# Products ahead of the transposes in each step of the first stack's attention

## The reference

```
proj = rms_norm(h, g_mix[l]) @ w_in[l];  q, k, v, xr, gr = split(proj)
# 4 heads, each with two score maps c = 0, 1 of head size 64; rotary on q and k
s = q_c @ k_c.T * 64**-0.5, causal;  pr = softmax(s)
attn = pr[0] - lam * pr[1];  o = attn @ v;  o = rms_norm(o, g_subln) * (1 - lam_init)
y = rg_lru(conv(xr)) * gelu(gr)                       # the recurrent half
h = h + concat([o, y]) @ w_out[l]
h = h + square(relu(rms_norm(h, g_mlp[l]) @ w_mlp_in[l])) @ w_mlp_out[l]
gate = sigmoid(rms_norm(h, g_ple[l]) @ w_ple_gate[l]);  h = h + gate * (p[l] @ w_ple_proj[l])
```

## Time and profile before

| | |
|---|---|
| median of 3 runs | 2460.05 us (2459.33 to 2461.67) |
| the profiled execution: its time | 2455.17 us |
| its span, first to last instruction | 2453.4 us |
| PE busy | 2394.1 us, 98% |
| PEld busy | 1937.7 us, 79% |
| DVE busy | 1362.2 us, 56% |
| ACT busy | 895.8 us, 37% |
| share of PE in the chain that ended last | 89% |
| attention steps of layer 0, 136.00 to 204.00 us: PE, DVE, ACT busy | 62.37, 45.33, 39.10 of 68.00 us, granted clock 1.00 |

### The profile page before, as it was taken

How to read it: one execution, slowest core, us unless ns; L and a number is a source line. 1 busy time by engine, 2 the same in 40 slices (tenths; PEclk the granted TensorE clock), 3 DMA queues, 4 the chain that set the end, 5 groups by cost and what they waited for, 6 DMA issues and landing times.

```text
span 2453.4 us, 28925 instructions
## 1 busy us (share of the span) xinstructions
PE 2394.1 (98%) x11498; PEld 1937.7 (79%) x11498; DVE 1362.2 (56%) x1976; ACT 895.8 (37%) x1299; POOL 349.9 (14%) x270
## 2 busy tenths in 40 slices
PE   8999999999999999999999999999999999999997
PEld 6877888888887788888876878888886877888886
DVE  7775433445777543344578876344357975633433
ACT  4555332234355533223432354223243244321331
POOL 2002000001200200000246521000012832000002
PEclk9999999999999999999999999999999999999998
DMA  4311222222231222222221221222221211222221
GB/s 158 107 57 69 98 91 103 91 98 86 102 109 56 74 102 87 103 94 89 91 91 69 69 84 59 103 93 95 102 104 57 87 52 70 81 91 103 91 97 51
DMA packets 33181, 215.56 MB, mean 88 GB/s; under 512 B 4145, under 2 KB 4401, under 8 KB 8113
## 3 DMA queue, kind: packets, MB, share of 16 engines
q1 hardware_dynamic: 33072, 214.08, 24.4%
HBM read 211.97 MB, written 2.10 MB: 87 GB/s over the span
## 4 chain that ended last, share of the span: by engine, by line
PE 89%; DVE 7%; ACT 2%; issue 1%; POOL 1%; DMA 0%; SPq 0%; POOLq 0%; DVEq 0%; ACTq 0%
PE ps L426 81%; DVE wl L366 1%; PE ps L2225 1%; PE ps L2178 1%; DVE gl L648 1%; PE ps L2249 1%; PE ps L2239 1%; PE ps L1389 1%; PE ps L606 1%; PE ps L1413 1%; PE ps L309 1%; PE ps L1376 1%; ACT wh L360 0%; PE ps L2228 0%; DVE x L1340 0%
## 5 line engine op out<-in xcount | busy, mean ns | idle before, releaser
L426 PE MATMUL ps<-gh,wh 128*128 128x512 f32 x1488 | 589.4, 396 | 13.6 <-DVE gl L648 11.0
L426 PE MATMUL ps<-gh,wl 128*128 128x512 f32 x1488 | 581.0, 390 | 0.0
L426 PE MATMUL ps<-gl,wh 128*128 128x512 f32 x1488 | 580.9, 390 | 0.0
L426 PE MATMUL ps<-hh,wh 128*128 128x512 f32 x1456 | 575.1, 395 | 3.0 <-ACT arena L964 1.1
L360 ACT ACTIVATE wh<-wr 128x2048 fp32r<-128x2048 f32 x184 | 351.1, 1909 | 594.9 <-PE ps L426 594.5
L426 PE MATMUL ps<-hh,wl 128*128 128x512 f32 x1456 | 567.3, 390 | 0.0
L426 PE MATMUL ps<-hl,wh 128*128 128x512 f32 x1456 | 567.0, 389 | 0.0
L366 DVE TENSOR_TENSOR wl<-wr,wh 128x2048 fp32r<-128x2048 f32 x168 | 387.1, 2304 | 277.8 <-ACT wh L360 275.5
L426 PEld LDWEIGHTS ps<-gh,wh 128*128 128x128 f32 x1488 | 279.3, 188 | 82.1 <-DVE gl L648 13.5
L426 PEld LDWEIGHTS ps<-hh,wh 128*128 128x128 f32 x1456 | 272.9, 187 | 68.3 <-issue 8.0
L426 PEld LDWEIGHTS ps<-gh,wl 128*128 128x128 f32 x1488 | 279.5, 188 | 59.7
(11 more groups left out here) (264 smaller groups left out, 2445.8 us busy)
## 6 DMA issues: line engine op xcount, KB each, us to landing
wr<-in_weights SPq DMA_DIRECT2D x195, 1024.0 KB, 4.8
out_yt<-x SPq DMA_DIRECT2D x8, 256.0 KB, 2.0
x<-in_xt SPq DMA_DIRECT2D x3, 512.0 KB, 7.9
wr<-in_weights SPq DMA_DIRECT2D x2, 512.0 KB, 5.8
arena<-in_gates SPq DMA_DIRECT2D x2, 512.0 KB, 7.7
arena<-in_embed SPq DMA_DIRECT2D x2, 512.0 KB, 5.3
par<-in_params_b SPq DMA_DIRECT2D x2, 274.0 KB, 2.7
x<-in_xt SPq DMA_DIRECT2D x2, 256.0 KB, 4.1
```

The costliest lines, as they stand in the source:

```text
L426: done = pe.matmul(out, stationary, moving, start=(first and n == 0), stop=(last and n == 2), skip_group_check=True)
```

## The change

In the loop over the 16 steps, PE's `recurrent_tile` or `projection_tile` is issued ahead of `turn(s)` (and of `turn_back`) instead of behind them. `scores(s+2)` stays first, `weigh(s-1)` last. The loop stands in the program of both first-stack layers. Nothing on the other engines changes its order.

```
         for s in range(STEPS):
             if s + 2 < STEPS:
                 scores(s + 2)
-            turn(s)
-            if s % QT == 3 and s > QT:
-                turn_back(s // QT - 1, s - 1)
             if s < KT:
                 recurrent_tile(s)
             else:
                 projection_tile(s - KT)
+            turn(s)
+            if s % QT == 3 and s > QT:
+                turn_back(s // QT - 1, s - 1)
             if s:
                 weigh(s - 1)
         weigh(STEPS - 1)
```

## The result

The changed kernel takes 2470.54 us (median of 5 runs, 2469.24 to 2471.19), the one before 2459.33 us (median of 5 runs, 2456.95 to 2461.67). The ratio is 1.0043, with a 95% interval of 1.0032 to 1.0054: slower by 8 to 13 us. Repeated on two chips, beside new runs of before, the same kernel gave 1.0034 twice (1.0021 to 1.0046, and 1.0022 to 1.0045). Forecast were 2468.5 us (a loss of 8.4) and a range of 2463.5 to 2473.

A forecast was written before the change was run, and what follows sets the result against it. PE, busy for 98% of the span, was taken as the bound. Per layer -5.1 - 0.96 - 0.07 + 5.9 + 3.7 = +3.5 us; two layers +7.1, with new neighbours +8.4, on 2460.05 gives 2468.5 us, range 2463.5 to 2473.

The forecast's parts named there:

- Part 1: At PE's transposes of the mixed probabilities: all waits for DVE's mix go, saving 5.1 us per layer.
- Part 2: At weigh in steps 7, 11, 15: PE stands 1.96 us each while bank 7 is emptied, 5.9 us per layer.
- rival 2: Faster: in steps 7, 11, 15 the bank 7 chain shrinks below 0.9 us; 2452.5 us, chance 0.04.
- Part 3: Projection tiles in steps 10, 11, 14, 15 wait for ACT's copy of an earlier tile: 3.7 us per layer.
- Rival 1: Only bank 7 costs, the projection copies stay hidden: +1.0 us, 2461 us, chance 0.12.
- Part 4: Transposes now ahead of 128x128 work in all 32 steps: 0 to 0.08 us each, 1.3 us taken in all.
- The sum: Both layers' steps: +3.5 us per layer, +7.1 for two, +8.4 us with the cost of new neighbours.
- slower by over 0.2%: Whole kernel: the outcome of a loss above 4.9 us, given a chance of 0.81.
- within 0.2%: Whole kernel: the outcome of a difference under 4.9 us, hard to tell from no change, chance 0.15.
- Rival 3: ACT sets the pace from step 8 on: 0.4 us for 8 steps per layer, +6.4 more, 2475 us, chance 0.09.
- Nothing later takes it up: Behind the steps: PE is bound by itself and no transfer depends on it, so the 8.4 us loss stays whole.

The follow-up runs named there:

- experiment 1: Changed kernel, but steps 7, 11 and 15 keep the old order, transposes ahead of products; 2459.74 us against 2459.16 before, ratio 1.0003.
- experiment 5: Kernel before with its PE order, but turn_back ahead of turn, and ACT's output_high and keep_projection ahead of untangle; 2456.44 us, ratio 0.9983.
- experiment 3: Changed kernel with turn_back ahead of the products in steps 7, 11, 15 and ACT's output_high ahead of untangle; 2455.72 us, ratio 0.9985.
- experiment 2: Changed kernel with ACT's keep_projection ahead of untangle instead of at the end of its step; 2467.30 us, ratio 1.003.
- experiment 4: Changed kernel with turn_back ahead of the products, and ACT's keep_projection, then output_high, ahead of untangle; 2452.84 us, ratio 0.9975, later 2453.85, ratio 0.9964.
- experiment 6: Changed kernel with turn_back ahead of the products in steps 7, 11 and 15, ACT's order left as it was; 2477.54 us, one run.
- the kernel filled in part: Changed kernel plus unread matmuls: 7 behind turn_back, 4 ahead of the projection tiles of steps 14 and 15; 2467.44 us, unfilled copy 2470.83.

## Why the prediction was right

**Part 1, waits that go (5.1 us per layer).** Right: no wait of L1401 is left in either layer. Experiments 1 and 5 bring it back exactly where the old order is.

**Part 2, bank 7 (1.96 us in each of three steps).** Right: 2.31 us from L1422 to L1413 again, less 0.35, with brackets of 1.71. Experiment 1 gives the three steps their old order and the loss is gone, experiment 3 hides the chain and 6.1 us per layer come back (75.11 to 69.02). The chain did not shrink, so rival 2 is refuted: no piece of it had been lateness.

**Part 3, the projection's copy (3.7 us per layer).** Right in place and size. Lost from start to start: step 10, 183.59 - 182.83 - 0.09 = 0.67 (0.65 was forecast); step 11, 0.45 (0.5); step 14, 200.42 - 198.87 - 0.31 = 1.24 (1.35); step 15, 203.96 - 202.24 - 0.54 = 1.18 (1.2). Together 3.5 us. The 0.09 is what the mask matmul now leaves to L426 where PE doesn't wait. Rival 1, in which these copies stay hidden, is refuted by experiment 2, whose brackets vanish.

**Part 4, new neighbours (1.3 us in all).** The steps in which PE waits for nothing measure it. The first scores of steps 1 and 2 in the changed kernel:

```profile
140.93 1.13 PE L1389 MATMUL ps<-arena 64*128 64x512 f32 x4
...
145.48 0.49 PE L1389 MATMUL ps<-arena 64*128 64x128 f32 x4
```

and before:

```profile
140.25 1.13 PE L1389 MATMUL ps<-arena 64*128 64x512 f32 x4
...
144.75 0.49 PE L1389 MATMUL ps<-arena 64*128 64x128 f32 x4
```

4.55 us instead of 4.50. In the same way steps 0, 2, 4, 5 and 6 are longer by 0.07, 0.05, 0.06, 0.08 and 0.01. The half of 0.08 that was taken is about right. The 0.08 itself was read from two groups that both stood behind a wait, but it holds where PE waits in neither kernel: two transposes take 0.14 us ahead of a 128x512 matmul (141.44 to 141.58, before) and 0.22 ahead of other 128x128 ones (144.94 to 145.16, changed), three take 0.26 and 0.33. Some 0.03 of it comes back behind the mask matmuls.

**The sum.** Forecast for the steps 8.4 us, measured 7.9 us. The chances don't follow from their own rule: 0.75 less a tenth of it, and 0.09, is 0.77 for "slower by over 0.2%" where 0.81 stands, and 0.19 is left for "within 0.2%" instead of 0.15. Rival 3 is refuted: scores wait once per layer for ACT, as before, and L1401 not at all.

**What the sum left out.** "Nothing later takes it up" named PE as bound by itself behind the steps, and took its speed as given. It is not: in each of the three traces of the changed kernel the granted clock falls behind the steps, in at least one layer. The medians are 11.2, 10.6 and 9.2 us above before in three comparisons, the means 11.2, 9.1 and 8.6: 0.7 to 3.3 us more than the steps. The range held this because the bounds of the other terms were wide, not because the clock was thought of; for this part it was luck.

That the rest is the clock can be read from the timed runs, since each has its mean granted clock on record. The 63 runs of before spread from 2455.2 to 2463.5 us, and the time follows the clock: 0.994 in the fast ones, 0.989 or 0.990 in the slow ones. Call (1 - clock) x time what a run loses by the clock, about 20 us in before. A straight line through all 157 timed runs that have a clock, with a level of its own for each kernel in each comparison, gives 0.67 us of time for each us of this loss. At equal clock the kernels then lie where their steps put them, to about 0.5 us (the clocks on record are rounded to 0.001, which is 2.5 us in one run, and the first set of the changed kernel is set against all runs of before, since those beside it have no clock on record):

| | from before, at equal clock | twice the stretch's difference |
|---|---|---|
| changed, three sets of runs | +7.9, +8.3, +7.9 | +7.9 |
| experiment 1 | +0.1 | +0.4 |
| experiment 3 | -4.2 | -4.3 |
| experiment 4, two sets | -6.8, -6.6 | -6.7 |
| experiment 5 | -4.6 | -4.1 |

Why the changed kernel's clock is lower is shown less well. In traces of kernels that keep the three waits of 1.71 us or more (the changed one three times, experiments 2 and 6) the clock falls in or right behind the steps in five of five; in those without them (before, experiments 1, 3 and 5, experiment 4 twice) in one of six. But it is no rule that several waits are needed or enough. In experiment 2 one gap of 1.71 us, behind more than 8 us without any, was followed by a fall, and the same gap in the same step of the changed kernel was not. In the kernel filled in part the clock fell behind gaps of 0.67 and 1.11 us, which stand in before too, without a fall. The Trainium skill, TensorE: Matmul & The Clock Gate, section on a second HAM failure mode, describes such a PE, which idles briefly and often between groups of matmuls and swings between its clocks. The traces agree in so far as the clock fell to 1.2 GHz at 829.2 us behind five waits of 0.67 to 1.71 us. A look at the gaps that the parts 2 and 3 added up to would have called for that rule.

What stays open: what decides, from one execution to the next, whether the clock falls behind such waits, and how much of the 0.7 to 3.3 us is owed to the change and how much to the spread that every kernel here shows.

## What to carry to other kernels

Before independent work is moved ahead of a dependent step, look at what that work was hiding on its other side: here it lay between two users of one PSUM bank, and between an engine's copy and the next request for it. The gain was real, 1.3 us per layer, but it could be had only after the consumers' own order had been turned as well, so that finished work doesn't stand behind a blocked instruction. A wait on TensorE can cost more than the wait, since the clock may fall behind short gaps, and a stretch that is 1.3 us longer than expected is worth a look at the granted clock first. Where two kernels differ by less than the spread of one, compare them at equal granted clock.

## What the runs showed of the hardware

- Idle gaps of 0.7 to 1.7 us on PE, at times a single one of 1.71, were followed in some executions and not in others by the lower clock level (1.2 GHz) for 3.4 to 10.2 us, during which 128x512 matmuls started 0.43 us apart instead of 0.23. In the one trace with the gaps filled by idle matmuls the clock stayed at 2.4 GHz there.
- The spread of one kernel's times on one core (2455.2 to 2463.5 us for before) goes with its mean granted clock, 0.994 to 0.989.
- Seven unneeded 128x512 matmuls in a gap of 1.96 us changed neither the end of the wait nor the stretch (75.11 us both).
- Four 128x128 transposes ahead of other 128x128 work take 0.43 us where PE had not waited (171.70 to 172.13) and 0.49 where it had the earlier trace rows; ahead of a 128x512 matmul, behind a wait, 0.41. So both the neighbour and the wait before count.
